# First layer's recurrence: the lower halves of two projections' weights made by VectorE instead of GpSimd

## The reference, cut to what matters

```python
pl = hl @ w_in                       # includes u, v (for chunk_mlp) and g
def step(state, inp):                # gla_chunked, one chunk
    b = cumsum(log_f); diff = b[t] - b[s]; decay = where(mask, exp(min(diff, 0)), 0)
    scores = einsum('tk,sk,tsk->ts', q, k, decay)
    out = (q * exp(b)) @ state + scores @ v
    new_state = exp(b_last) * state + (k * exp(b_last - b)).T @ v
def chunk_mlp(u_pre, v_pre, ...):
    u = gelu(u_pre); v = rms_norm(gelu(v_pre))
    return u * (ws @ v + bs)         # over each chunk of 128 tokens
... (o * silu(g))                    # g is used in the stage after this one
```

## Time and profile before

| | before |
|---|---|
| median of 3 runs | 2647.91 us (2647.44 to 2651.93) |
| the profiled execution | 2654.73 us, its span 2653.0 us |
| PE busy | 2522.3 us (95%) |
| DVE busy | 1669.1 us (63%) |
| ACT busy | 988.7 us (37%) |
| POOL busy | 172.9 us (7%), of it 31.9 us in the 13 subtractions of this stage |
| granted TensorE clock, mean | 0.986 |

### The profile page before, as it was taken

One profiled execution on the slowest core, in us unless ns is written; L12 is line 12 of the kernel. 1 busy time (PEld: TensorE's weight loads), 2 busy tenths in 40 slices (PEclk: granted clock), 3 DMA queues, 4 the chain that ended last, 5 costly groups with the idle time before them and its releaser, 6 DMA issues. The chain is left out here.

```text
span 2653.0 us, 36362 instructions
## 1 busy us (share of the span) xinstructions
PE 2522.3 (95%) x14741; PEld 2128.3 (80%) x14741; DVE 1669.1 (63%) x2706; ACT 988.7 (37%) x1362; POOL 172.9 (7%) x183
## 2 busy tenths in 40 slices
PE   8999899999999999999999999999989998989997
PEld 3888787788888888866679989977778886867786
DVE  5887697566767776444446756737967775354744
ACT  4235555332212222345443323325542224345532
POOL 0111011000000000012000000001610000000000
PEclk9999999999999999999999999999999999999998
DMA  6650012223343333221023443322210001211232
GB/s 261 197 160 18 23 33 88 72 87 96 101 154 119 97 104 108 70 71 48 1 72 120 137 149 125 116 82 76 80 58 17 17 9 48 96 60 68 80 103 80
DMA packets 62425, 232.26 MB, mean 88 GB/s; under 512 B 6961, under 2 KB 9649, under 8 KB 61618
## 3 DMA queue, kind: packets, MB, share of 16 engines
q1 hardware_dynamic: 46962, 173.82, 19.9%
q0 software_dynamic: 15296, 56.11, 6.7%
HBM read 227.02 MB, written 2.10 MB: 86 GB/s over the span
## 5 line engine op out<-in xcount | busy, mean ns | idle before, releaser
L395 DVE TENSOR_TENSOR w_lo<-w_raw,w_hi 128x1024 fp32r<-128x1024 f32 (+2 forms) x253 | 323.0, 1277 | 322.9 <-ACT w_hi L339 318.7
L339 ACT ACTIVATE w_hi<-w_raw 128x1024 fp32r<-128x1024 f32 (+4 forms) x284 | 298.1, 1050 | 253.8 <-PE late_acc L485 93.3
L485 PE MATMUL mid_acc<-mid_h_hi,w_hi 128*128 128x258 f32 x832 | 279.4, 336 | 1.5 <-DVE mid_od_fq L653 1.0
L485 PE MATMUL mid_acc<-mid_h_hi,w_lo 128*128 128x258 f32 x832 | 279.0, 335 | 0.0
L485 PE MATMUL mid_acc<-mid_h_lo,w_hi 128*128 128x258 f32 x832 | 277.1, 333 | 0.0
L485 PE MATMUL late_acc<-late_h_hi,w_hi 128*128 128x258 f32 x704 | 199.3, 283 | 0.0
L485 PE MATMUL late_acc<-late_h_hi,w_lo 128*128 128x258 f32 x704 | 198.4, 282 | 0.0
L485 PE MATMUL late_acc<-late_h_lo,w_hi 128*128 128x258 f32 x704 | 197.7, 281 | 0.0
L485 PEld LDWEIGHTS mid_acc<-mid_h_hi,w_hi 128*128 128x128 f32 x832 | 157.3, 189 | 19.4 <-issue 2.4
L485 PEld LDWEIGHTS mid_acc<-mid_h_lo,w_hi 128*128 128x128 f32 x832 | 157.5, 189 | 18.6 <-issue 1.2
L485 PEld LDWEIGHTS mid_acc<-mid_h_hi,w_lo 128*128 128x128 f32 x832 | 156.8, 189 | 16.1
(11 more groups left out here) (527 smaller groups left out, 6169.8 us busy)
## 6 DMA issues: line engine op xcount, KB each, us to landing
w_raw<-in_up SPq DMA_DIRECT2D x88, 512.0 KB, 3.6
mid_side_raw<-in_ada_t POOLq DMA_DIRECT2D x48, 512.0 KB, 3.8
w_raw<-in_down SPq DMA_DIRECT2D x32, 704.0 KB, 4.1
qvz_side_raw<-in_ada_t POOLq DMA_DIRECT2D x32, 512.0 KB, 4.3
w_raw<-in_dn_qkv SPq DMA_DIRECT2D x25, 512.0 KB, 3.2
late_side_raw<-in_ada_t POOLq DMA_DIRECT2D x24, 512.0 KB, 4.1
w_raw<-in_da SPq DMA_DIRECT2D x18, 512.0 KB, 3.2
w_raw<-in_ev_qvz SPq DMA_DIRECT2D x16, 512.0 KB, 4.3
```

What stands on the lines that cost most here:

```text
L339: nc.scalar.activation(K.whi[:, g % 2, 0:width], K.raw[:, g % 2, 0:width], ACT.Copy).then_inc(K.hi_done, 1)
L395: nc.vector.tensor_tensor(K.wlo[:, g % 2, 0:width], K.raw[:, g % 2, 0:width], K.whi[:, g % 2, 0:width].bitcast(F32), ALU.subtract).then_in ...
L485: last = nc.tensor.matmul(self.acc[i % len(self.acc)][:, at:at + width], left[:, j, cols], right[k][:, moving:moving + width], start=((i, ...
```

## The change

The two flows no longer put their lower halves on GpSimd. `low_turns=[5]` puts the lower half of tile i+2 at turn 5 (the sixth of eight) of tile i's pass on VectorE, for all eight tiles of `uv` and all four of `evg`; the lower half of each flow's tile 1 is made by `first()`. The block has no GpSimd program any more. Nothing else moves; the order of all other instructions is the same, and so are the buffers and the DMAs.

```diff
         flow = Flow(K, c, "uv", A["ev_uv"], 2 * B_GROUPS, DT, h_hi, h_lo, 0, TOK,
                     [(1, cm.gelus)], [(2, cm.gate)],
-                    (A["ev_g"], DT), acc=acc, parts=2, low_on_pool=True)
+                    (A["ev_g"], DT), acc=acc, parts=2, low_turns=[5] * (2 * B_GROUPS))
...
         flow_g = Flow(K, c, "evg", A["ev_g"], A_HEADS, DT, h_hi, h_lo, 0, TOK, [(1, gates)], [], nxt, acc=acc, parts=2,
-                      after=flow, then=2, low_on_pool=True)
+                      after=flow, then=2, low_turns=[5] * A_HEADS)
...
-            @block.gpsimd
-            def _(pool):
-                flow.pool(pool)
-                flow_g.pool(pool)
-
```

## The result

| | before | after |
|---|---|---|
| median of 5 runs each | 2650.00 us (2647.44 to 2651.93) | 2660.21 us (2655.52 to 2666.64) |
| the profiled execution | 2654.73 us, its span 2653.0 us | 2659.92 us, its span 2658.1 us |
| from TensorE's first piece of the stage to the next stage's first VectorE instruction | 253.4 us | 261.7 us |
| granted TensorE clock, mean | 0.986 | 0.987 |

A forecast was written before the change was run, and what follows sets the result against it. TensorE bounds from 210 to 270 us, TensorE and VectorE both from 326 to 362. 6.8 + 0.3 + 1.4 - 0.7 = +7.8, clock +1.2, together +9.0: 2656.9 us; own range 2653.5 to 2659.5, wider 2650.0 to 2662.0.

The forecast's parts named there:

- The six places at the full price: Six lower halves on VectorE with no slack behind them: 1.14 us each, 6.8 us together.
- The four free ones: Four lower halves on VectorE hidden by idle time or other engines' waits: each claimed to cost 0.
- uv 1: Lower half ahead of `keys(0)`, on the first step's VectorE and ScalarE chain without slack: +1.14 us.
- uv 7 and evg 0: Two lower halves where TensorE and VectorE are full: 2.28 us less VectorE's idle time, +1.4 us.
- uv 3: Lower half ahead of a norm TensorE takes at once; VectorE's 0.84 us idle covers most: +0.3 us.
- evg 1: Lower half where VectorE newly waits 0.6 us for the upper half, covered by TensorE's gelu wait: 0.
- The interference: GpSimd's subtractions stretch six VectorE instructions: 10.3 us of VectorE's time returns, only 0.7 us on the path, before `update(9)`.
- (A): Rival, chance 0.14: the stretches were on the path; 2.8 us faster, 2645.1 us, or 9.2 faster, 2638.7 us.
- (B): Rival, chance 0.13: VectorE bounds the stage throughout, every addition and return counts; +4.5 us, 2652.4 us.
- (C): Rival, chance 0.13: three more clock falls (3.6 us) and 0.1 us per new wait; +12.7 us, 2660.6 us.
- The clock's term: One more fall of TensorE's clock in the stage, behind a lengthened wait: +1.2 us, bounds 0 to 3.6.
- Everything after it only shifted: Behind the stage, lengthened by 8 to 9 us, the rest of the kernel would only move later.

The follow-up runs named there:

- e4: Changed kernel with unused matmuls filling three TensorE waits (before the norms of groups 2 and 3 and `turn_keys(5)`); 2656.89 us, ratio 1.0022 to before.
- e5: Kernel before with unused matmuls in three TensorE waits, before the norms of groups 2 and 3 and `turn_keys(5)`; 2650.59 us, ratio 0.9991.
- e9: e4 with 33 more unused matmuls in TensorE's wait at the stage's start; 2653.17 us, ratio 1.0008 to before.
- e10: e5 with 30 more unused matmuls in TensorE's wait at the stage's start; 2647.81 us, ratio 0.9985 to before.
- a0: The changed kernel again, unaltered, on the same chip as other follow-up runs; 2662.55 us, ratio 1.0041 to before.
- e6: Kernel before, GpSimd making only 8 of 1024 columns of each of the 13 lower halves; 2653.47 us, ratio 1.0000 to before.
- e1: Kernel before with only the four lower halves forecast as free moved to VectorE, nine left on GpSimd; 2649.72 us, ratio 0.9990.
- e3: Changed kernel, all thirteen lower halves on VectorE but seven at other turns; 2656.22 us, ratio 1.0009 to before.
- e7: Changed kernel, VectorE making only 8 of 1024 columns of each lower half, waits kept; 2650.35 us, ratio 0.9992 to before.
- e8: e1's four lower halves on VectorE, plus unused matmuls in three waits and at the stage's start; 2645.96 us, ratio 0.9979 to before.

## Why the prediction was right

**The number, and what of it is luck.** +9.0 us was forecast, and the medians lie 10.2 us apart (+9.5 by the ratio). The time itself, 2660.21 us, is 3.3 above the 2656.9 and above the forecast's own band, 2653.5 to 2659.5; 2.1 of that come from the median of before, 2647.91 in three runs and 2650.00 in five. The two parts of the sum came out differently in the whole kernel. With the waits filled the medians lie 6.3 (e4, e5) and 5.4 us (e9, e10) apart, and without 10.2 and 9.9 (a0). So some 4 us go with the clock, where I had 1.2, and 5 to 6 with the places, where I had 7.8: the errors offset each other. The runs of one kernel lie up to 14 us apart (e9: 2649.95 to 2664.07), so this split is rough. What is shown closely is the price of the places inside the stage.

**The place decides, and each place came out.** The table of e9 less e10 is the prediction's sum row by row: 7.23 us measured, 7.8 forecast. The six places at the full price gave 1.21, 3.28 for three, 1.14 and 1.13. The four free ones gave nothing to within 0.02 us where the table can see them (uv 2 lies in the first row together with uv 1). Two terms were too large. *uv 7 and evg 0*, 1.05 instead of 1.4: I took off VectorE's idle time before `update(5)` and a like one before `update(6)`, 0.83 together, and the slack was 1.2; VectorE's idle time before the two updates, 0.40 and 0.39 us in e10, is gone in e9, and where the other 0.4 lies I haven't found. *uv 3*, 0.18 instead of 0.3.

**uv 1 was right in price, but in the first profile of after hardly shows.** TensorE's wait grew by 0.63 us only (7.73 to 8.36), for VectorE had stood 1.53 us for the masks in before and 0.99 in after: the DMA landed sooner against the stage. And `update(0)` comes at the same distance from the start, 47.3 us in both, since the slow stretch at the start was shorter (0.80 to 0.86). With the clock full in e9 and e10 the 1.21 are there.

**evg 1, the new wait**, stood 0.51 us for the upper half (0.6 forecast) and cost 0.01: the cover was TensorE's own wait of 1.75 us for ScalarE's gelu, which is 1.75 in after too.

**The interference.** 10.3 us forecast and 10.3 measured as VectorE's time; 0.7 forecast and 0.78 to 0.79 measured on the path (e6, e9 less e10). The Trainium skill ("SBUF — State Buffer", section "Who interferes with whom") told rightly that the two engines shut each other out, and e6 shows both sides of it: the stretches go when GpSimd's reads shrink, and the end doesn't move. The large form of (A), all 10.3 us on the path, was my reading and not the page's. As a reason for this change the interference was worth a thirteenth of what it seemed.

**The rivals.** (A), the stretches on the path, fell by e6. (B), VectorE bounds throughout, fell by e1 and e3: four lower halves on VectorE cost nothing in the one, and in the other all thirteen are there and the three waits of TensorE that their places spare are before's. Of (C) the part with a price for each wait on top of the 1.14 us fell by e7 and by the table, where no row but uv 1 is over its forecast by more than 0.02 us; the 0.1 us a wait that (C) put there had no source in the traces before. The other part, that the clock falls more often, isn't refuted: its 3.6 us are nearer than my 1.2 to the some 4 us by which the medians differ with the waits filled and unfilled. No profile gives it as a number, since one kernel gave +8 and +14 us with equal waits.

**The clock's term** was right in sign for the median and wrong in its picture. I had one more fall, +1.2 us, behind a lengthened wait. In the first profile of after there was a long one at 331 us (`update(4)` to `update(5)` takes 3.5 us more than in before, of which 0.5 are uv 7), the clock from 210 to 326 us was 0.97 for 0.99, and the falls at the start and near 366 us, which before had, were shorter or gone. In sum +8.3 us of the stage against 7.2 with the clock left out, so the term was 1.1 us in that pair, by luck near 1.2. What failed is the rule that I read from before, that the length of a wait tells whether a fall follows. The wait ahead of `turn_keys(5)` is 2.31 to 2.33 us in before, e1, e3, e6 and e7; from 326 to 362 us before was granted 1.00 and the four others 0.95, 0.91, 0.91 and 0.95. So the row that the forecast rested on, 2.32 us and no fall, was the exception of the five. The wait of 1.75 us for the gelu was followed by a fall in before and in e8, and by none in after and in e10.

**"Everything after it only shifted"** was wrong for the profiled pair: the offset fell from 8.0 to 5.4 us at some 1250 us, by a fall of the clock in before that after doesn't have. Nothing that was changed is near. The profiled executions differ by 5.2 us and the medians by 10.2, and the reason for looking at the stage alone is there.

## What to carry to other kernels

Price an added instruction by what is queued behind it: where the next result of that engine ends a wait of the bounding one it costs its full length less the idle time of its own engine ahead of that result, elsewhere nothing, and the same table says which of the moved pieces are worth keeping (here four of thirteen). A gain in busy time, as the end of an interference, is to be followed to the end of the path in the same way: of 10.3 us 0.8 arrived. And where TensorE's clock falls inside the stage that is compared, fill its waits in both kernels before you compare; a difference of the stage that was blurred by several us then agreed with the sum, step by step, to 0.4 us or better. It holds for the stage: what the rest of the kernel makes of it has to be looked at by itself (here 7.2 us in the stage and 5.4 between the medians).

## What the runs showed of the hardware that was not expected

The falls of TensorE's clock in the middle of the stage are dearer than I took them for, and cheap to avoid: with unused matmuls in four waits, e10's stage is 6.0 us shorter than before's (253.4 to 247.4), and its time 0.15% below (ratio 0.9985, 0.9976 to 0.9993). The same program, with equal waits to 0.05 us, was granted 0.91 in one execution and 0.81 in another from 326 to 362 us, and its stage differed by 5.7 us. And VectorE's subtraction of 128x1024 took 1.22 us where GpSimd's took 2.35 to 2.65.
